# Eight bursts of eight one-hot groups in place of sixteen bursts of four, in a PEER layer on one Trainium2 core

## The reference, cut to what matters

```python
def _peer(xn, w_q, k1, k2, u_tab, v_tab):
    ...
    top_v, top_c = lax.top_k(cand, PEER_TOPK)
    e1 = jnp.take_along_axis(i1, top_c // PEER_TOPK, axis=-1)
    e2 = jnp.take_along_axis(i2, top_c % PEER_TOPK, axis=-1)
    idx = e1 * N_KEYS + e2
    gates = jax.nn.softmax(top_v, axis=-1).astype(xn.dtype)
    ...
        u = u_tab[ib]
        act = jax.nn.gelu(jnp.einsum('phkd,pd->phk', u, xb), approximate=False)
        return jnp.einsum('phk,phkd->pd', gb * act, v_tab[ib])
```

## Time and profile before

| what | value |
|---|---|
| median of 3 runs | 1452.13 us (1451.76 to 1453.65) |
| profiled execution, its own time | 1451.17 us |
| its span in the profile | 1449.4 us |
| PE busy | 1442.9 us |
| PEld busy | 1203.1 us |
| DVE busy | 1122.8 us |
| ACT busy | 766.5 us |
| POOL busy | 446.2 us |
| HBM traffic | 345.16 MB by DMA, mean 238 GB/s |
| gate stage, first to last gate matmul | 674.6 to 898.2 us of the span |

### The profile page before, as it was taken

The page is one execution under the profiler, slowest core; times in us unless marked ns, Lnnn a source line. Parts: engine busy times, 40 slices in busy tenths (PEclk is TensorE's granted clock), DMA queues, the critical chain, the costliest instruction groups (busy, mean ns, idle before and its releaser), DMA issues.

```text
span 1449.4 us, 22294 instructions
## 1 busy us (share of the span) xinstructions
PE 1442.9 (100%) x7422; PEld 1203.1 (83%) x7422; DVE 1122.8 (77%) x1926; ACT 766.5 (53%) x1008; POOL 446.2 (31%) x209
## 2 busy tenths in 40 slices
PE   9999999999999999999999999999999999999999
PEld 8888887878888888888888888888888888888887
DVE  5979898876699999996999996356666666666665
ACT  7445787676645455554655555454444444444442
POOL 5867566347457778882000000000000000000000
PEclk9999999999999999999999999999999999999999
DMA  7544534457433666666888888979988898888893
GB/s 246 171 145 145 189 117 153 168 190 259 146 137 119 218 218 216 216 215 217 305 298 308 301 305 298 338 243 323 295 285 291 288 292 287 289 290 291 287 290 138
DMA packets 166706, 345.16 MB, mean 238 GB/s; under 512 B 13420, under 2 KB 78956, under 8 KB 164336
## 3 DMA queue, kind: packets, MB, share of 16 engines
q1 hardware_dynamic: 166640, 344.32, 69.8%
HBM read 268.76 MB, written 75.51 MB: 238 GB/s over the span
## 4 chain that ended last, share of the span: by engine, by line
PE 97%; DVE 1%; ACT 1%; DMA 1%; issue 0%; POOL 0%; SPq 0%; POOLq 0%; ACTq 0%
PE ps L1296 32%; PE ps L1305 32%; PE ps L796 13%; PE ps L819 6%; PE ps L1334 4%; PE ps L1167 2%; PE ps L1006 1%; PE ps L784 1%; PE ps L1231 1%; PE ps L1016 1%; PE ps L1060 1%; PE ps L1238 1%; PE ps L868 1%; DMA w_raw<-in_w 1%; PE ps L1188 1%; PE ps L844 0%
## 5 line engine op out<-in xcount | busy, mean ns | idle before, releaser
L1296 PE MATMUL ps<-hT_r,u_r 128*128 128x512 f32 x2048 | 470.3, 390 | 0.0
L1305 PE MATMUL ps<-v_r,w_pairs 128*128 128x512 f32 x2036 | 461.7, 389 | 0.0
L1296 PEld LDWEIGHTS ps<-hT_r,u_r 128*128 128x128 f32 x2048 | 382.9, 188 | 79.0
L1305 PEld LDWEIGHTS ps<-v_r,w_pairs 128*128 128x128 f32 x2036 | 382.3, 188 | 79.2
L2487 DVE TENSOR_TENSOR v_r<-vraw,v_r 128x1024 fp32r<-128x1024 f32 x128 | 156.9, 1226 | 148.1 <-ACT v_r L1805 148.1
L1805 ACT ACTIVATE v_r<-vraw 128x1024 fp32r<-128x1024 f32 x128 | 135.8, 1061 | 253.6 <-PE ps L1305 248.6
L506 POOL TENSOR_TENSOR w_r<-w_raw,w_r 128x1024 fp32r<-128x1024 f32 x85 | 222.6, 2625 | 151.5 <-ACT w_r L1413 105.1
L586 POOL TENSOR_TENSOR u_r<-uraw,u_r 128x1024 fp32r<-128x1024 f32 x60 | 173.7, 2908 | 41.3 <-ACT u_r L1732 41.1
L1751 ACT ACTIVATE act_stage<-ps 128x512 f32<-128x512 f32 x128 | 76.5, 598 | 181.2 <-PE ps L1296 181.1
L1732 ACT ACTIVATE u_r<-uraw 128x1024 fp32r<-128x1024 f32 x128 | 135.3, 1058 | 53.8 <-DMA uraw<-in_u 53.4
L1413 ACT ACTIVATE w_r<-w_raw 128x1024 fp32r<-128x1024 f32 x95 | 100.0, 1059 | 84.9 <-PE ps L819 33.1
(11 more groups left out here) (301 smaller groups left out, 1579.3 us busy)
## 6 DMA issues: line engine op xcount, KB each, us to landing
uraw<-in_u SPq DMA_DIRECT2D x128, 512.0 KB, 4.7
vraw<-in_v SPq DMA_DIRECT2D x128, 512.0 KB, 5.2
w_raw<-in_w SPq DMA_DIRECT2D x100, 512.0 KB, 3.4
acts_out<-act_stage SPq DMA_DIRECT2D x128, 256.0 KB, 2.3
gates<-stage SPq DMA_DIRECT2D x16, 2048.0 KB, 7.4
g_in<-gates SPq DMA_DIRECT2D x64, 512.0 KB, 6.5
act_in<-acts_out SPq DMA_DIRECT2D x128, 256.0 KB, 5.2
gates_pre<-pre_stage SPq DMA_DIRECT2D x24, 256.0 KB, 2.3
```

The lines of the kernel that those rows point to most:

```text
L1296: ins = pe.matmul(bank(s % 2), u2[s][:, w, k * P:(k + 1) * P], hr4[:, w, k, :], start=i == 0, stop=i == 15, skip_group_check=True)
L1305: ins = pe.matmul(bank(2 * q + h), w2[:, s, w, q * P:(q + 1) * P], v2[s][:, w, h * BANK:(h + 1) * BANK], start=start and w == 0, stop=stop ...
```

## The change

TensorE runs eight groups in one burst and then six up products, so there are eight bursts in the stage in place of sixteen. Within a burst the pairs of PSUM banks go round as 0, 1, 2, 0, 1, 2, 0, 1. ScalarE's and VectorE's orders follow, SyncE stores both halves of the staging buffer ahead of the loads and spills of the six tiles, and the last list is turned two up products earlier. The number of instructions that compute stays the same.

```diff
-EXP_AFTER, TURN_AFTER = (12, 24, 36, 49), (23, 36, 48, 56)
+EXP_AFTER, TURN_AFTER = (12, 24, 36, 49), (23, 36, 48, 54)
+BURST, BURST_UPS = 8, 6
...
                 for b in range(4):
-                    tile(3 * b)
+                    if b % 2 == 0:
+                        load_tile(3 * b)
                     sp.wait_ge(gate_out, j * 16 + 4 * (b + 1))
                     sp.dma_start(gates_dram[j * 4 + b], stage[:, b % 2 * NKEYS * BLK:(b % 2 + 1) * NKEYS * BLK]
                                  ).then_inc(block_stored[b % 2], 16)
-                    tile(3 * b + 1)
-                    tile(3 * b + 2)
+                    if b % 2:
+                        for m in range(3 * b - 3, 3 * b + 3):
+                            if m > 3 * b - 3:
+                                load_tile(m)
+                            spill(j * PER_BLOCK + (N_TOP + m), m % 4)
...
             def gate_group(g, s):
 
                 pe.wait_ge(oh_ready, g + 1)
-                at_least(pe, gate_out, g if s % 4 == 0 else g - 2)
+                at_least(pe, gate_out, g if s == 0 else g - 2)
                 for q in range(GT):
                     for w in range(2):
-                        at = (2 + 2 * (s % 4 % 3)) * BANK + q * P
+                        at = (2 + 2 * (s % 3)) * BANK + q * P
...
-                for b in range(4):
-                    for i in range(4 * b, 4 * b + 4):
-                        gate_group(j * 16 + i, i % 8)
-                    for m in range(3 * b, 3 * b + 3):
+                for b in range(2):
+                    for i in range(BURST):
+                        gate_group(j * 16 + (b * BURST + i), i)
+                    for m in range(b * BURST_UPS, (b + 1) * BURST_UPS):
                         up(j * PER_BLOCK + (N_TOP + m), m % 4)
...
-                for b in range(4):
-                    at_least(act, block_stored[b % 2], j * 32 + (b // 2) * 16)
-                    n = j * PER_BLOCK + (N_TOP + 3 * b)
-                    for i in range(4 * b, 4 * b + 4):
+                for b in range(2):
+                    m = b * BURST_UPS
+                    n = j * PER_BLOCK + (N_TOP + m)
+                    for i in range(b * BURST, (b + 1) * BURST):
+                        if i % 4 == 0:
+                            at_least(act, block_stored[i // 4 % 2], j * 32 + b * 16)
                         gate_copy(j * 16 + i, i)
                         if i % 4 == 1:
-                            high_u(n + 2, (3 * b + 2) % 4)
-                    gelu(n, 3 * b % 4)
-                    high_u(n + 3, (3 * b + 3) % 4)
-                    gelu(n + 1, (3 * b + 1) % 4)
-                    high_u(n + 4, (3 * b + 4) % 4)
-                    gelu(n + 2, (3 * b + 2) % 4)
+                            d = 2 + i % BURST // 4
+                            high_u(n + d, (m + d) % 4)
+                    for d in range(BURST_UPS):
+                        gelu(n + d, (m + d) % 4)
+                        if d < BURST_UPS - 2:
+                            high_u(n + (d + 4), (m + d + 4) % 4)
```

More of the change, by code:

```diff
@@ L718, in gate_blocks, with load_tile @@
             def gate_blocks(j):
[L720 to L723, removed]
+                def load_tile(m):
+                    load_u(j * PER_BLOCK + (N_TOP + m + 4), m % 4)
                 for b in range(4):
-                    tile(3 * b)
+                    if b % 2 == 0:
+                        load_tile(3 * b)
                     sp.wait_ge(gate_out, j * 16 + 4 * (b + 1))
@@ L1775, in gate_copy @@
                 act.activation(stage4[:, i // 4 % 2, :, (i % 4) * GT:(i % 4 + 1) * GT],
-                               bank(2 + 2 * (i % 4 % 3), 2).rearrange("p (q k) -> p k q", k=NKEYS),
+                               bank(2 + 2 * (i % BURST % 3), 2).rearrange("p (q k) -> p k q", k=NKEYS),
                                ACT.Copy).then_inc(gate_out, 1)
             def gate_blocks(j):
-                for b in range(4):
-                    at_least(act, block_stored[b % 2], j * 32 + (b // 2) * 16)
-                    n = j * PER_BLOCK + (N_TOP + 3 * b)
-                    for i in range(4 * b, 4 * b + 4):
+                for b in range(2):
[4 more added lines that the diff above has]
+                            at_least(act, block_stored[i // 4 % 2], j * 32 + b * 16)
                         gate_copy(j * 16 + i, i)
                         if i % 4 == 1:
-                            high_u(n + 2, (3 * b + 2) % 4)
-                    gelu(n, 3 * b % 4)
-                    high_u(n + 3, (3 * b + 3) % 4)
-                    gelu(n + 1, (3 * b + 1) % 4)
-                    high_u(n + 4, (3 * b + 4) % 4)
-                    gelu(n + 2, (3 * b + 2) % 4)
+                            d = 2 + i % BURST // 4
[4 more added lines that the diff above has]
+                            high_u(n + (d + 4), (m + d + 4) % 4)
             act.wait_ge(list_ready, TT)
@@ L2450, in low_u, with between_bursts, gate_blocks @@
                                   ALU.subtract).then_inc(u_lo_dve, 1)
[L2452 to L2467, removed]
+            def between_bursts(j, b):
+                m = b * BURST_UPS
+                n = j * PER_BLOCK + (N_TOP + m)
+                g = j * 16 + (b + 1) * BURST
+                low_u(n + 1, (m + 1) % 4)
+                one_hots(g, 0)
+                low_u(n + 2, (m + 2) % 4)
+                one_hots(g + 1, 1)
+                one_hots(g + 2, 2)
+                low_u(n + 3, (m + 3) % 4)
+                one_hots(g + 3, 3)
+                low_u(n + 4, (m + 4) % 4)
+                one_hots(g + 4, 4)
+                low_u(n + 5, (m + 5) % 4)
+                one_hots(g + 5, 5)
+                one_hots(g + 6, 6)
+                low_u(n + 6, (m + 6) % 4)
+                one_hots(g + 7, 7)
+            def gate_blocks(j):
+                between_bursts(j, 0)
+                between_bursts(j, 1)
+            for g in range(BURST):
+                one_hots(g, g)
+            low_u(N_TOP, N_TOP % 4)
             gate_blocks(0)
@@ L2470, in _ @@
                 gate_blocks(j)
-            gate_blocks(NBLK // 4 - 1, 3)
-            for n in range(N_GATE - 2, N_GATE + 1):
+            between_bursts(NBLK // 4 - 1, 0)
+            for n in range(N_GATE - 5, N_GATE + 1):
                 low_u(n, n % 4)
```

## The result

The changed kernel takes 1460.51 us (median of 6 runs, 1459.88 to 1463.10) where the kernel before took 1451.95 in the same comparison: a ratio of 1.006 with a 95% interval of 1.0047 to 1.0073, 8.6 us more where 10.5 were forecast. The profiled execution took 1461.38 us, its span is 1459.6, 10.2 above that of before.

A forecast was written before the change was run, and what follows sets the result against it. TensorE was taken as the bound, busy 1442.9 of 1449.4 us. Terms -0.7 (fewer bursts), +4.0 (copies) and +7.2 (late load) gave +10.5 us, a median of 1462.6 us, range 1454.0 to 1472.0.

The forecast's parts named there:

- Eight bursts fewer: Gate stage, TensorE: each burst costs 0.09 us beyond its own work, so eight fewer save 0.7 us.
- The copy stall: Within each burst, group 5 waits for ScalarE's copy of group 2: 0.5 us a burst, +4.0 us.
- The late load: Sixth tile's load, behind two stores, delays ScalarE's GELU and the fifth up product: 0.9 us a burst, +7.2 us.
- the threshold: Latest landing of the sixth tile's load that costs TensorE nothing: T+20.8, with T the burst's start.
- the load is in time: Rival: stores pass faster or the load slips between them, leaving only the copy stall; 1455.4 us, chance 0.22.
- The start: Ahead of the first burst: last list turned earlier, eight one-hot sets ready by 679 us, TensorE does not wait, cost nothing.
- no wait of TensorE for VectorE: Sign expected in the changed kernel's profile: VectorE's one-hot sets are ready in time, with cover of 4.7 us.
- The clock: Rival: short TensorE waits lower the granted clock, up to 59 us more, 1522 us; chance 0.03.

The follow-up runs named there:

- dve_makes_58_59: Changed kernel, but VectorE instead of GpSimd makes the low parts of tiles 58 and 59, between its first one-hot sets: 1461.15 us in one execution.
- high_behind_copies: Changed kernel, but ScalarE makes a burst's two high parts behind the fifth and sixth copy: 1457.97 us, ratio 1.0045 to the kernel before.
- load_between_stores: Changed kernel, but SyncE issues the sixth tile's load between the two stores: 1456.24 us, ratio 1.0039 to the kernel before.
- load_before_spill: Changed kernel, but the sixth tile's load, still behind both stores, goes ahead of the first tile's spill: 1457.82 us in one execution.
- turn_at_56: Changed kernel, but the last list is turned after the up product of tile 56, as before the change: 1462.71 us in one execution.
- start_mended: Changed kernel, load between stores, high parts behind copies five and six, VectorE making low parts 58, 59 and, before the seventh set, 60: 1450.84 us, ratio 0.9996.

## Why the prediction was right

*Eight bursts fewer, -0.7 us:* the sign was right and the size too small. With every wait removed two periods went from 29.34 to 29.19 us, 0.15 a burst, 1.2 us in all.

*The copy stall, +4.0 us:* 0.50 us in each burst from the third on, 0.56 in the second. In the first burst VectorE's late set hides it, and it shows there, 0.58 us long, once the set is in time (dve_makes_58_59). The forecast put the sixth group at T+5.1, and it began at T+5.06. high_behind_copies shows the cause.

*The late load, +7.2 us:* the chain of causes was right, and load_between_stores and load_before_spill show it, but the size was taken evenly and is not even. I put the load at T+21.7 and the threshold at T+20.8. It came at T+21.2 twice, at T+20.4 to 20.7 in the last five periods, and the threshold was T+20.6, as the burst is 7.8 us and not 8.0 long. So it cost 0.6 us twice, 0.15 twice, nothing three times, and 3.05 us once. The term measured 4.6 us in waits, 3.05 of them in the first period, where the forecast had 0.9; the seven others, for which it had 6.3, show 1.5. What was mis-sized in most of them is the second store: I gave it 6.1 us at the rate of a mixed window, while the two landed 5.1 to 5.2 apart in each of the last five periods, at T+12.4 and T+17.5 in the one at 770.95. In the second and third they were 6.2 and 6.9 apart, and there 0.6 us of the 0.9 forecast came. The Trainium skill's figure (DMA: Bandwidth & Descriptors, section Bandwidth, 425 GB/s for a transfer of 16 MB, there measured for loads) comes nearer to the five: 2.1 MB in 5.1 us are 411 GB/s. In these five periods the rival "the load is in time" is what happened, or within 0.15 us of it.

*The start, "nothing":* this step failed, and with it the sign "no wait of TensorE for VectorE". I gave the eight sets 2.53 to 2.65 us each and had them complete by 679; they were complete at 682.8, 4.3 us of it from the two instructions that stood beside GpSimd's low parts. I had looked at GpSimd's slack and not at what GpSimd does to VectorE. The Trainium skill has the rule (SBUF — State Buffer, section Terms, the shared port pair): VectorE and GpSimd take turns at one pair of ports, locked for a whole instruction, and "the loser **fully blocks**". The trace agrees: 2.76 and 2.88 us, ending 0.54 us after GpSimd. It cost 1.0 us within the first burst and 0.2 at an up product behind it, and delayed `low_u` of tile 60, behind which SyncE held the load of tile 64 and the first store till T+9.2 in place of T+6.2. The stores landed at T+17.9 and T+23.0, 5.5 us later than in a late period, and the load at T+24.7. How much of the 3.05 us is this step's is not shown: dve_makes_58_59, with no long one-hot instruction and the first store at T+7.2, still got the load at T+24.5 and waited longer. Only beside the other two edits did mending the start pay, 32.17 to 29.60 us for the period.

*The clock, 0.03:* a rival that came true in a small part. Behind the 0.5 us waits, which were feared, the clock stayed at 1.00. It was the wait of 3.05 us in the first period of the profiled execution that was followed by the slow intervals, 1.3 us; those of 3.2 us in high_behind_copies and 3.85 in dve_makes_58_59 were too, 1.6 us each, and in turn_at_56 so were three waits of 1.0 to 1.7 us within the first burst. After 2.28 us in load_before_spill the clock stayed at 1.00. Not every execution of the changed kernel need have lost this time: the three whose mean granted clock was 1.000 took 1459.88 to 1460.25 us, the three with 0.999 or 0.998, the profiled one among them, 1460.77 to 1463.10.

So 4.0 + 7.2 - 0.7 = 10.5 were forecast, and the profiled execution shows 4.1 (copies, with the 0.58 us of the first burst counted here) + 4.6 (GELU) + 1.3 (clock) + 1.2 (late sets) - 1.2 (bursts) = 10.0 in the stage. Its periods add up to 9.5, as the weight loads behind a gap make up some of it, and the other 0.7 of the 10.2 lie ahead of the stage. Two of the five terms were not in my sum, and they about make up for the overrated load; and of the load's 4.6 us, two thirds fell in a period with its own late start. The copy stall was foreseen; that the total came so close is luck.

## What to carry to other kernels

Grouping work into longer bursts saves only what the joints really cost, here 0.15 us each, while it takes up the slack of every buffer that turns over within a burst or between two: bank pairs, the order on ScalarE, the DMA queue behind a double store. Before moving work earlier on VectorE, look at what GpSimd does in that stretch. And ask first how large the gain could be with every wait mended: here all edits together only bring the kernel back to where it was, within what can be measured.

## What was not expected of the hardware

One-hot instructions of 0.69 us took 2.76 and 2.88 us beside GpSimd's subtractions, whose own 2.4 us became 2.68 and 2.60, and none was long in the three runs in which GpSimd was done before they began (turn_at_56, dve_makes_58_59, start_mended). Two stores of 2 MB back to back landed 5.1 us apart, 411 GB/s, in five of eight periods, over the 346 GB/s of a stretch with loads and spills mixed in; in two others it was 6.2 and 6.9 us. A load queued behind them landed 2.9 us after the second store with one 0.25 MB spill between.
